# A transformer-and-experts block on one core: weights of the first group fetched early, scale and shift applied after the transpose, and the 16 copies of h2 at a block's start placed elsewhere

## The chip, the cores and the metric

The kernel runs on one core of a Trainium2 chip. TensorE (PE) multiplies, VectorE (DVE) and ScalarE (ACT) work on tiles in on-chip memory, GpSimd (POOL) starts the gathers, and SyncE (SP) starts all other transfers in the order in which they stand in its program. The metric is device microseconds of one execution, lower is better.

## The reference, cut to what matters

The block has one layer, a sequence of 1024 rows, width 1024, all in float32:

```python
mod = jax.nn.silu(c) @ w_ada + b_ada
shift1, scale1, gate1, shift2, scale2, gate2 = jnp.split(mod, 6, axis=-1)
h = rmsnorm(x, norm1_g) * (1 + scale1) + shift1
proj = h @ w_in          # stick-breaking q|k|v, sliding-window q|k|v, two gates
x = x + gate1 * (merged @ w_out)
h2 = rmsnorm(x, norm2_g) * (1 + scale2) + shift2
x = x + gate2 * peer_ffn(h2, ...)   # per row and head (8): top 16 of 16384 experts
return rmsnorm(x, final_g)

# peer_ffn, per block of 128 rows
act = gelu(einsum('td,thkd->thk', h2, expert_u[experts]))
out = einsum('thk,thkd->td', gate * act, expert_v[experts])
```

## The kernel before, in words

There are two kinds of work. The **mixer** (everything up to h2 and the scores of the experts' keys) runs over three groups of 2, 3 and 3 blocks of 128 rows. The stages of a group are called H (norm, modulation, transposes), V, QK and SB (four pairs of heads of the stick-breaking branch), SWP and SW (the window branch), MG (the gated merge, eight tiles of weights w_mg), OUT (w_out, gate1, h2) and PREP (eight heads of w_q and sub-keys sk, whose scores pick the experts).

The **expert stream** runs over 8 blocks of 128 tiles each, 1024 in all. A tile is one gather (line 530) of 128 rows of 2048 floats, 1 MB, into a ring of 10 slots. For each tile DVE forms 128 dot products with a copy of h2 (line 1411). For each quad of 4 tiles ACT takes gelu (1100) and spreads the weights over `dg` (1106), and PE sums (880) into the PSUM pair VACC. That sum, counted by `vs_done`, frees four slots, and POOL may start gathers again. A tile is 32 rows of the block by 4 experts, so `h2rep` holds in its part c the rows 32c to 32c+31 of h2, four times over the partitions. It is made anew for each block from `h2cur` in 16 steps, c = 0 to 3 by i = 0 to 3 (a quarter of the width each), each four matmuls of PE (866) and one copy of ACT (1084), which wait for each other step by step because both use one half of PSUM bank MISC. The first dot product of a block with part c needs the four copies of that c. `publish` (848, 1068, 1070) turns the picked experts into indices and gates, 32 tiles at a time, through the other half of MISC. `final` (1421 to 1431) takes a block's sum out of VACC.

Every engine's program is one straight list. It is made by `interleave`, which merges streams by the number that each `yield` gives: in the expert stream this number is the tile's, in the mixer it comes from `Plan`. Group 0 of the mixer lies at negative numbers, so it runs ahead of the first tile; groups 1 and 2 are mixed into the tiles from 0 on. A wait in one stream holds up all that stands behind it on that engine.

The modulation vector is computed in three rounds (546) from `w_ada`, 8 MB each, that go through the ring's memory, before the ring is in use. Rows scale1 and shift1 go out to HBM and come back spread over 128 partitions, and DVE applies them to the rows (1164, 1165) ahead of the transposes (564).

Of the kernel before, what the change touches and what calls it, by code (L numbers as in the profile page):

```python
# [185 lines left out]
def build(nc, x, c8, w_ada, b_ada, g1, g2, gf, w_v, w_qk, w_sw, sinks, w_mg, w_out, w_q, sk, uv, consts,  # L186
          x1_dram, h2_dram, mods_dram, k_dram, v_dram, s_dram, out):
    with ExitStack() as ctx:
# [72 lines left out]
        wqk = [rows(X0, 2 * KT, P), rows(L0, 2 * KT, P)]  # L261
# [3 lines left out]
        wsw = rows(W0, 6 * KT, P).rearrange("p (a k) n -> p a k n", a=6)  # L265
# [14 lines left out]
        wq = [rows(W0 + 2048 * i, 2 * KT, P).rearrange("p (a k) n -> p a k n", a=2) for i in range(2)]  # L280
        skt = [rows(W0 + 4096 + 256 * i, 2, NKEYS) for i in range(2)]
# [9 lines left out]
        in_rows1, in_rows2, in_rowsf = sem("in_rows1"), sem("in_rows2"), sem("in_rowsf")  # L291
# [3 lines left out]
        in_wqk = [sem("in_wqk0"), sem("in_wqk1")]  # L295
# [45 lines left out]
        with nc.Block() as block:  # L341
            @block.sync
            def _(sp):
                def start():
# [28 lines left out]
                def mixer(g):  # L373
# [1120 lines left out]
```

## Time and profile before

| | us |
|---|---|
| median of 3 runs (lowest, highest) | 3668.83 (3667.49, 3670.41) |
| the profiled execution, own time | 3687.68 |
| its span, first to last instruction | 3685.9 |
| busy: PE, weight loads, DVE, ACT, POOL | 2249.2, 996.8, 2036.1, 1144.6, 1121.7 |
| gathers started | 1024 |
| moved by DMA in all | 1276.13 MB, mean 346 GB/s |

Only one profile exists; its own time stands 18.85 us above the median of the runs. Idle time of an engine is shown in brackets with what ended it.

### The profile page before, as it was taken

To read this page: it belongs to the slowest core of one execution; us is meant where nothing else is said; L and a number is where in the kernel's file an instruction comes from. 1 tells how busy PE (TensorE), PEld (TensorE's weight loads), DVE (VectorE), ACT (ScalarE), POOL (GpSimd) and SP (SyncE) were. 2 spreads that over 40 slices of the span, in tenths; PEclk is the share of its full clock that TensorE was granted. 3 is DMA by queue.
4 is the path that set the end of the run, shared out by engine and by line. 5 is a ranking of instruction groups with operands and counts; after the bars stand their busy time and mean duration, and the time that the engine had idled before them with its cause. 6 is when DMAs were issued, how large, how long until landed. Compare 5 with 4: busy or idle time off the path is not lost.

```text
span 3685.9 us, 35795 instructions
## 1 busy us (share of the span) xinstructions
PE 2249.2 (61%) x11240; PEld 996.8 (27%) x11240; DVE 2036.1 (55%) x4768; ACT 1144.6 (31%) x3633; POOL 1121.7 (30%) x1033
## 2 busy tenths in 40 slices
PE   4678766875987856777667877684433343334333
PEld 2466623333443422223233332241000000000000
DVE  1011445657456455677577665656566656665644
ACT  1210124634213233666634213222222222222221
POOL 0000112332223323344233333333344434433432
PEclk8889868887988978888787988796555555655565
DMA  6424558888799998999899998999799989997998
GB/s 262 169 77 160 188 215 315 330 346 320 316 392 384 373 397 327 370 399 400 318 385 371 421 422 328 393 420 420 309 415 421 421 315 421 421 421 307 421 421 336
DMA packets 196264, 1276.13 MB, mean 346 GB/s; under 512 B 21261, under 2 KB 38701, under 8 KB 54633
## 3 DMA queue, kind: packets, MB, share of 16 engines
q0 software_dynamic: 147616, 1074.03, 71.8%
q1 hardware_dynamic: 48456, 199.80, 14.1%
q8 instruction: 89, 1.46, 0.2%
q14 instruction: 103, 0.84, 0.1%
HBM read 1249.35 MB, written 24.40 MB: 346 GB/s over the span
## 4 chain that ended last, share of the span: by engine, by line
PE 38%; DMA 33%; ACT 10%; issue 10%; DVE 6%; POOL 1%; another core or an unknown queue 1%; SPq 0%; POOLq 0%; DVEq 0%; ACTq 0%
DMA arena<-in_uv,idx_r 25%; PE pb L880 12%; PE pb L600 4%; PE pb L665 3%; ACT dg L1106 3%; PE pb L866 3%; PE pb L685 2%; PE pb L629 2%; ACT L104 2%; PE pb L603 2%; DVE arena L1411 2%; DMA arena<-in_w_q 2%; POOL arena L530 1%; PE pb L759 1%; DMA arena<-in_w_out 1%
## 5 line engine op out<-in xcount | busy, mean ns | idle before, releaser
L530 POOL DMA_INDIRECT arena<-in_uv,idx_r x1024 | 1118.6, 1092 | 2536.6 <-PE pb L880 1857.3
L1411 DVE CUSTOM_DVE_ANT_0 arena<-arena 128x1024 f32<-128x1024 f32 x1024 | 1247.8, 1221 | 719.9 <-DMA arena<-in_uv,idx_r 713.1
L880 PE MATMUL pb<-arena,dg 128*32 128x512 f32 x4096 | 745.1, 865 | 892.0 <-ACT dg L1106 842.6
L880 PEld LDWEIGHTS pb<-arena,dg 128*32 128x32 f32 x4096 | 134.6, 138 | 1395.5 <-ACT dg L1106 1033.7
L1100 ACT ACTIVATE gl<-dots 128x4 f32<-128x4 f32 x256 | 52.3, 204 | 1044.8 <-DVE dots L1411 1021.1
L665 PE MATMUL pb<-arena 128*128 128x384 f32 (+1 forms) x768 | 252.9, 487 | 57.3 <-issue 38.0
L104 ACT ACT_TABLE_LOAD x176 | 225.8, 1283 | 141.6 <-DVE dots L1411 68.4
L600 PE MATMUL pb<-arena 128*128 128x384 f32 (+1 forms) x768 | 241.5, 471 | 22.1 <-DMA arena<-in_w_mg 22.1
L1106 ACT ACTIVATE dg<-ig,gl 128x32 f32<-128x32 f32 x1024 | 245.1, 310 | 8.3
L1095 ACT ACTIVATE ig<-istack,gate_r 128x32 f32<-128x32 f32 x1024 | 241.5, 308 | 0.0
L665 PEld LDWEIGHTS pb<-arena 128*128 128x128 f32 x768 | 154.7, 206 | 150.3 <-issue 80.9
L600 PEld LDWEIGHTS pb<-arena 128*128 128x128 f32 x768 | 149.5, 198 | 117.5 <-issue 53.3
L866 PE MATMUL pb<-arena,ident 128*32 128x256 f32 x1024 | 106.7, 498 | 95.8 <-ACT arena L1084 87.1
L685 PE MATMUL pb<-arena 128*128 128x384 f32 (+1 forms) x384 | 127.4, 490 | 44.7 <-DMA arena<-in_w_qk 44.7
L629 PE MATMUL pb<-arena 128*128 128x512 f32 x256 | 121.6, 629 | 50.5 <-DMA arena<-in_w_out 47.7
L1277 DVE SCALAR_TENSOR_TENSOR arena<-pb,arena 128x384 f32<-128x384 f32 (+2 forms) x120 | 51.4, 470 | 153.0 <-ACT arena L1033 148.4
L603 PE MATMUL pb<-arena 128*128 128x384 f32 (+1 forms) x384 | 116.0, 454 | 0.0
L685 PEld LDWEIGHTS pb<-arena 128*128 128x128 f32 x384 | 77.7, 208 | 97.9 <-DMA arena<-in_w_qk 47.3
L713 PE MATMUL pb<-arena,tri 128*128 128x384 f32 (+2 forms) x240 | 93.5, 483 | 16.2 <-DVE arena L1277 15.1
L1084 ACT ACTIVATE arena<-pb 128x256 f32<-128x256 f32 x128 | 49.1, 384 | 147.3 <-PE pb L866 141.7
L1237 DVE SCALAR_TENSOR_TENSOR arena<-arena,pb 128x384 f32<-128x384 f32 (+1 forms) x48 | 24.3, 507 | 125.5 <-PE pb L603 125.2
L727 PE MATMUL pb<-arena 128*64 128x384 f32 (+2 forms) x240 | 67.0, 517 | 41.7 <-ACT arena L1041 39.1
(153 smaller groups left out, 2239.9 us busy)
## 6 DMA issues: line engine op xcount, KB each, us to landing
arena<-in_w_mg SPq DMA_DIRECT2D x24, 1536.0 KB
arena<-in_w_ada SPq DMA_DIRECT2D x12, 2048.0 KB, 17.7
arena<-in_w_q SPq DMA_DIRECT2D x24, 1024.0 KB
arena<-in_uv,idx_r POOLq DMA_INDIRECT x1024
arena<-in_w_qk SPq DMA_DIRECT2D x12, 1024.0 KB
arena<-in_w_out SPq DMA_DIRECT2D x3, 4096.0 KB, 16.3
arena<-in_w_sw SPq DMA_DIRECT2D x3, 3072.0 KB, 13.4
arena<-in_x SPq DMA_DIRECT2D x16, 512.0 KB, 20.8
```

The source lines that it names most:

```text
L104: self.act.add_instruction(mybir.InstLoadActFuncSet(name=self.nc.get_next_instruction_name(), act_func_set_id=table, engine=mybir.EngineTy ...
L530: pool.indirect_dma_start(ring[:, i % RING, :], None, uv, bass.IndirectOffsetOnAxis(ap=idx_r[:, b % 2, 4 * n + c:4 * n + c + 1], axis=0)). ...
L600: m = pe.matmul(bank, wmg[ft % 2][:, q * KT + k, :], hT[:, k, 0:T], start=(k == 0), stop=(k == KT - 1))
L603: m = pe.matmul(bank, wmg[ft % 2][:, 16 + (q - 2) * 4 + k, :], y[:, k, 0:T], start=(k == 0), stop=(k == 3))
L629: m = pe.matmul(pb[:, BGB + 2 * (j % 2) + i, :], merged[:, k, j * P:(j + 1) * P], wout[:, k, i * HALF:(i + 1) * HALF], start=(k == 0), sto ...
L665: m = pe.matmul(pb[:, BGB + p, 0:T], wq[h % 2][:, p, k, :], h2T[:, k, 0:T], start=(k == 0), stop=(k == KT - 1))
L685: m = pe.matmul(pb[:, BGB + i, 0:T], wqk[p % 2][:, i * KT + k, :], hT[:, k, 0:T], start=(k == 0), stop=(k == KT - 1))
L866: x_ = pe.matmul(pb[32 * q:32 * q + 32, MISC, 256:512], selector(c), h2cur[:, 256 * i:256 * i + 256], start=True, stop=True)
L880: m = pe.matmul(pb[32 * c:32 * c + 32, VACC + i, :], dg[:, STEP * n // 4 % 2, c, :], ring[:, (STEP * g + c - first) % RING, D + i * HALF:D ...
L1095: op = act.activation(ig[:, half, first + c], istack[:], ACT.Copy, scale=gate_r[:, b % 2, STEP * n + c:STEP * n + c + 1])
L1106: op = act.activation(dg[:, half, first + c], ig[:, half, first + c], ACT.Copy, scale=gl[:, a + c:a + c + 1])
L1411: dve.tensor_tensor_reduce(u, h2rep[:, c, :], u, 1.0, 0.0, ALU.mult, ALU.add, dots[:, i % 8:i % 8 + 1]).then_inc(dots_done, 1)
```

## The change

- Weights of group 0 go to places in the ring's memory (`RINGO + ...`), which is empty until the first gather, and are fetched by `first_weights` and `start`: w_v and w_qk 0 to 2 at the start, w_sw, two w_mg, w_out during the pairs, a third w_mg, w_q and sk at SW. For groups 1 and 2 the homes are as before.
- w_ada comes in halves by k, x between them in round 0. Rounds 1 and 2 of the modulation stand one pair earlier on PE.
- scale1 and shift1 are transposed on PE into a small tile `cols`. ACT scales the rows by the norm's factor (three copies of 1024), and the evacuation of the transposes applies scale and shift: four instructions of 128 columns in place of one copy of 512, on ACT and on DVE. The row loads of scale1 and shift1 go in all three groups.
- Scores for the first top-16 are copied on DVE out of `ssb`, not through HBM.
- For block 0, h2rep is loaded by four DMAs from HBM in stage OUT; its 16 steps are gone.
- For blocks 1 to 7 the 16 steps have other numbers, on PE -2.9 + 1.5c + 0.37i and on ACT -2.4 + 1.5c + 0.37i from the block's first tile (before: -3.6 and -3.5, + c + 0.1i). DVE's `final` stands ahead of the next block's first dot product, not behind it.

```diff
                     yield -2000
...
+                    for k in range(2):
+                        for c in range(2):
+                            ada(0, k, c)
+                        if k == 0:
+                            for j in range(SIZE[0]):
+                                sp.dma_start(xt[:, j, :], x[j * P:(j + 1) * P, :]).then_inc(in_x[j], 16)
+                    sp.dma_start(f(W0, 4096), w_v).then_inc(in_wv, 16)
+                    for p in range(3):
+                        sp.dma_start(f(qk_home(0, p), 2048), w_qk[p]).then_inc(in_wqk[p], 16)
...
+                def first_weights():
+                    yield at("QK", 0, 0, 0.3)
+                    sp.wait_ge(v_mm, SIZE[0])
+                    sp.dma_start(f(qk_home(0, 3), 2048), w_qk[3]).then_inc(in_wqk[3], 16)
+                    yield at("QK", 0, 2, -1)
+                    sp.wait_ge(ada_mm, 3)
+                    sp.dma_start(f(sw_home(0), 6144), w_sw).then_inc(in_wsw, 16)
+                    sp.wait_ge(qk_mm, 2)
+                    sp.dma_start(alibi, consts[:, 2 * P + TOPK + 32:2 * P + TOPK + 32 + TABLE]).then_inc(in_alibi, 16)
+                    merge_weights(0, 0)
+                    merge_weights(0, 1)
+                    yield at("QK", 0, 3)
+                    sp.wait_ge(qk_mm, 6)
+                    sp.dma_start(f(out_home(0), 8192), w_out).then_inc(in_wout, 16)
+                    yield at("SW", 0, 0)
+                    sp.wait_ge(sw_mm, 6)
+                    merge_weights(0, 2)
+                    query_weights(0, 1)
...
                 def blocks():
-                    for b in range(NB):
+                    yield at("OUT", 0, 0, 16.5)
+                    sp.wait_ge(h2_st[0], 16)
+                    sp.wait_ge(mods_out, 128)
+                    for q in range(4):
+                        sp.dma_start(h2rep[32 * q:32 * q + 32, :, :], h2_dram[0:P, :].rearrange("(c t) n -> t c n", c=4)).then_inc(in_rep, 16)
+                    for b in range(1, NB):
                         yield TILES * b - 24
...
-                        yield at("H", 0, 0, -2) if r == 0 else at("QK", 0, 2 * r - 1, -0.01)
+                        yield at("H", 0, 0, -2) if r == 0 else at("QK", 0, r - 1, -0.01)
...
-                                yield TILES * b - 3.6 + c + 0.1 * i if b else -2
+                                yield TILES * b - 2.9 + 1.5 * c + 0.37 * i
...
-                                yield TILES * b - 3.5 + c + 0.1 * i if b else -2
+                                yield TILES * b - 2.4 + 1.5 * c + 0.37 * i
...
+                    for j in range(GB):
+                        act.activation(xt[:, j, :], xt[:, j, :], ACT.Copy, scale=stats[:, 8 + j:9 + j]).then_inc(h_rows, 1)
...
+                        for k in range(4):
+                            op = act.activation(hT[:, k, j * P:(j + 1) * P], pb[:, BGB + 2 * (j % 2), k * P:(k + 1) * P], ACT.Identity,
+                                                scale=cols[:, 2 + k // 4, k % 4:k % 4 + 1], bias=cols[:, k // 4, k % 4:k % 4 + 1])
...
-                        link(dve.scalar_tensor_tensor(out=xt[:, j, :], in0=xt[:, j, :], scalar=stats[:, 8 + j:9 + j], in1=sc1_row, op0=ALU.mult, op1=ALU.mult))
-                        dve.tensor_tensor(xt[:, j, :], xt[:, j, :], sh1_row, ALU.add).then_inc(h_rows, 1)
...
                     for b in range(NB):
-                        yield TILES * (b + 1) + 0.9
+                        yield TILES * (b + 1) - 0.05
                         dve.wait_ge(vs_done, STEPS * (b + 1))
```

**SP in group 0, from pair 1's k on.** v_scratch to arena is the values of a pair (vp), which its scores wait for. Before:

```order
L418 DMA k_scratch<-arena 128x256
L423 DMA arena<-in_w_sw 128x6144
L424 DMA arena<-in_consts 128x1536
L431 DMA arena<-in_w_mg 128x3072 x8
L370 DMA arena<-mods_scratch 128x1024
L371 DMA arena<-in_gf 128x1024
L434 DMA arena<-in_w_out 128x8192
```

and of the change:

```order
L476 DMA k_scratch<-arena 128x256
L408 DMA arena<-in_w_sw 128x6144
L410 DMA arena<-in_consts 128x1536
L431 DMA arena<-in_w_mg 128x3072 x2
L469 DMA arena<-v_scratch 128x256
L476 DMA k_scratch<-arena 128x256
L469 DMA arena<-v_scratch 128x256
L415 DMA arena<-in_w_out 128x8192
L476 DMA k_scratch<-arena 128x256
L431 DMA arena<-in_w_mg 128x3072
L434 DMA arena<-in_w_q 128x2048
```

w_sw and two w_mg now stand ahead of the values of pair 2, and w_out behind those of pair 3.

**PE at the start of block 7**, 880 being the sums before (961 now), 866 the steps of h2rep (947 now) and 848 the publishing (929 now). Before:

```order
L880 MATMUL pb<-arena,dg 32x512 x56
L866 MATMUL pb<-arena,ident 32x256 x16
L880 MATMUL pb<-arena,dg 32x512 x8
L866 MATMUL pb<-arena,ident 32x256 x16
L848 MATMUL pb<-picks,ident 32x16 x16
L866 MATMUL pb<-arena,ident 32x256 x32
L880 MATMUL pb<-arena,dg 32x512 x64
```

and of the change, 4 matmuls to a step:

```order
L961 MATMUL pb<-arena,dg 32x512 x64
L947 MATMUL pb<-arena,ident 32x256 x12
L929 MATMUL pb<-picks,ident 32x16 x16
L947 MATMUL pb<-arena,ident 32x256 x28
L961 MATMUL pb<-arena,dg 32x512 x8
L947 MATMUL pb<-arena,ident 32x256 x24
L961 MATMUL pb<-arena,dg 32x512 x56
```

Before, 4 steps stood ahead of the sum of the last quad but one and 12 behind it, all ahead of the last quad's sum. Now none stands ahead of the former; 10 stand ahead of the last quad's sum and 6 behind it.

**ACT at the same place**, 1084 being the copies of the steps (1176 now), 1100 and 1106 the last quad's gelu and spreading (1192 and 1198 now). Before:

```order
L1084 ACTIVATE arena<-pb 128x256 x4
L104 ACT_TABLE_LOAD
L1062 ACTIVATE best<-best 128x32
L1084 ACTIVATE arena<-pb 128x256
L1095 ACTIVATE ig<-istack,gate_r 128x32 x4
L1084 ACTIVATE arena<-pb 128x256 x3
L1068 ACTIVATE idx_r<-pb 128x4x8
L1070 ACTIVATE gate_r<-pb 128x4x8
L1084 ACTIVATE arena<-pb 128x256 x8
L104 ACT_TABLE_LOAD
L1100 ACTIVATE gl<-dots 128x4
L1106 ACTIVATE dg<-ig,gl 128x32 x4
```

and of the change:

```order
L1176 ACTIVATE arena<-pb 128x256 x3
L1162 ACTIVATE idx_r<-pb 128x4x8
L1164 ACTIVATE gate_r<-pb 128x4x8
L1176 ACTIVATE arena<-pb 128x256 x4
L104 ACT_TABLE_LOAD
L1192 ACTIVATE gl<-dots 128x4
L1198 ACTIVATE dg<-ig,gl 128x32 x4
L1176 ACTIVATE arena<-pb 128x256 x4
L1187 ACTIVATE ig<-istack,gate_r 128x32 x4
L1176 ACTIVATE arena<-pb 128x256 x3
L1205 ACTIVATE arena,stats<-arena 128x1024
```

The last quad's gelu stood behind all 16 copies; it now stands behind 7, and 9 follow it.

## Rows read from the trace of the kernel before

**Rows 1.** The page, chain that ended last: share of the span by engine.

```profile
PE 38%; DMA 33%; ACT 10%; issue 10%; DVE 6%; POOL 1%; another core or an unknown queue 1%; SPq 0%; POOLq 0%; DVEq 0%; ACTq 0%
```

**Rows 2.** Windows: busy us by engine, then clock (1 is full), DMA share, GB/s.

```profile
474.00:532.00 58.00, 26.92 (x173) 8.99 (x172) 20.84 (x45) 17.21 (x43) 0.00 (x0) 0.54 0.29 117
2700.00:2800.00 100.00, 36.01 (x192) 6.30 (x192) 67.66 (x156) 22.95 (x94) 38.05 (x38) 0.57 1.01 421
3335.00:3435.00 100.00, 38.82 (x228) 7.07 (x224) 58.95 (x137) 29.09 (x99) 33.01 (x32) 0.52 0.85 341
```

**Rows 3.** Timeline of PE to 540 us: start, us, what, [idle before <-releaser].

```profile
29.32 9.54 PE L546 MATMUL pb<-arena,cb 128*32 128x512 f32 x64 [29.32 <-DMA arena<-in_w_ada]
...
58.75 15.41 PE L576 MATMUL pb<-arena 128*128 128x512 f32 x32 [0.87 <-DVE arena L1168]
80.81 9.49 PE L685 MATMUL pb<-arena 128*128 128x256 f32 x32 [6.65 <-DMA arena<-in_w_qk]
...
134.94 9.73 PE L685 MATMUL pb<-arena 128*128 128x256 f32 x32 [13.39 <-DMA arena<-in_w_qk]
...
185.60 16.90 PE L759 MATMUL pb<-arena 128*128 128x256 f32 x64 [10.03 <-DMA arena<-in_w_sw]
...
245.17 9.22 PE L600 MATMUL pb<-arena 128*128 128x256 f32 x32 [6.35 <-DMA arena<-in_w_mg]
...
257.68 7.07 PE L600 MATMUL pb<-arena 128*128 128x256 f32 x32
...
344.29 29.74 PE L629 MATMUL pb<-arena 128*128 128x512 f32 x64 [13.93 <-DMA arena<-in_w_out]
...
390.78 9.79 PE L665 MATMUL pb<-arena 128*128 128x256 f32 x32 [6.36 <-DMA arena<-in_sk]
...
531.70 5.89 PE L576 MATMUL pb<-arena 128*128 128x512 f32 x12
```

**Rows 4.** Source view of the four first w_ada loads: us from issue to landing.

```profile
L354 SPq DMA_DIRECT2D arena<-in_w_ada x4: 423/432/432, 4.9 to 6.4; - x4
...
DMA to landing us min/median/max: 9.5/16.2/22.8
```

**Rows 5.** DMA view: two groups of weights, KB each, median us to landing.

```profile
arena<-in_w_mg SPq DMA_DIRECT2D x24, 1536.0 KB
...
arena<-in_w_sw SPq DMA_DIRECT2D x3, 3072.0 KB, 13.4
```

**Rows 6.** Timeline between group 0 and group 1, DVE, PE and ACT.

```profile
419.60 0.29 DVE L1309 MAX8 vals<-arena 128x8 f32<-128x128 f32 x1 [34.44 <-DMA arena<-s_scratch]
...
443.68 0.49 PE L848 MATMUL pb<-picks,ident 128*32 128x16 f32 x32 [4.15 <-DVE picks L1385]
...
481.07 1.06 ACT L904 ACTIVATE arena<-arena 128x1024 f32<-128x1024 f32 x1 [6.27 <-DMA arena<-in_x]
...
508.43 0.38 ACT L1084 ACTIVATE arena<-pb 128x256 f32<-128x256 f32 x1 [1.20 <-PE pb L866]
...
508.83 1.28 ACT L104 ACT_TABLE_LOAD   x1
```

**Rows 7.** Source view of the copies into h2rep: ns min/median/max, first and last start.

```profile
L1084 ACT ACTIVATE arena<-pb x128: 358/384/387, 484.7 to 3345.2; 128x256 f32<-128x256 f32 x128
```

**Rows 8.** Timeline at the start of block 7, POOL, ACT and PE.

```profile
3309.95 0.94 POOL L530 DMA_INDIRECT arena<-in_uv,idx_r  x1 [4.96 <-PE pb L880]
...
3317.64 0.38 ACT L1084 ACTIVATE arena<-pb 128x256 f32<-128x256 f32 x1 [1.35 <-DVE dots L1411]
...
3326.18 1.88 POOL L530 DMA_INDIRECT arena<-in_uv,idx_r  x1 [11.56 <-PE pb L880]
...
3348.18 3.64 PE L880 MATMUL pb<-arena,dg 128*32 128x512 f32 x16 [3.01 <-ACT dg L1106]
...
3352.66 0.94 POOL L530 DMA_INDIRECT arena<-in_uv,idx_r  x1 [20.88 <-PE pb L880]
...
3367.77 1.57 POOL L530 DMA_INDIRECT arena<-in_uv,idx_r  x1 [9.62 <-PE pb L880]
```

More of the change, by code:

```diff
@@ L279, in build, with qk_home, sw_home, mg_home @@
         h2T = merged
[L280 to L281 removed]
         qp = rows(W0 + 4608, 2, TMAX)
         ssb = [f(W0 + 4608 + 2 * TMAX * (i + 1), 2 * TMAX).rearrange("p (b q n) -> p b q n", b=GMAX, q=2) for i in range(2)]
+        def qk_home(g, p):
+            return (X0, RINGO + 16384, RINGO + 18432, L0)[p] if g == 0 else (X0, L0)[p % 2]
+        def sw_home(g):
+            return RINGO if g == 0 else W0
+        def mg_home(g, ft):
+            return RINGO + (6144, 9216, 0)[ft % 3] if g == 0 else W0 + 3072 * (ft % 2)
+        def mg_turn(g, ft):
+            if g == 0:
+                return ft % 3, ft // 3 + 1
+            return ft % 2, 3 + KT // 2 * (g - 1) + ft // 2 + 1
+        def out_home(g):
+            return RINGO + 12288 if g == 0 else A0
+        def q_home(g, h):
+            return RINGO + 3072 if (g, h) == (0, 1) else W0 + 2048 * (h % 2)
+        def sk_home(g, h):
+            return (RINGO + 5120 if g == 0 and h < 2 else W0 + 4096) + 256 * (h % 2)
         dve_steps, pool_steps = sem("dve_steps"), sem("pool_steps")
@@ L357, in mods @@
                 def mods():
-                    for r in range(3):
-                        yield at("H", 0, 0, -0.5) if r == 0 else at("QK", 0, 2 * r - 1, 0.5)
+                    for r in range(1, 3):
+                        yield at("H", 0, 0, 1) if r == 1 else at("QK", 0, 0, 0.6)
+                        sp.wait_ge(ada_mm, r)
+                        for k in range(2):
+                            for c in range(2):
+                                ada(r, k, c)
+                        yield at("QK", 0, r - 1, 0.5)
@@ L506, in finals @@
                         sp.dma_start(out[b * P:(b + 1) * P, :], yfin).then_inc(stored, 16)
-                interleave(start(), mods(), mixer(0), parked(0), keys(), blocks(), finals(), *[s for g in range(1, GROUPS) for s in (mixer(g), parked(g))])
+                interleave(start(), mods(), first_weights(), mixer(0), parked(0), keys(), blocks(), finals(), *[s for g in range(1, GROUPS) for s in (mixer(g), parked(g))])
                 sp.wait_ge(stored, 16 * NB)
@@ L548, in modulation @@
                         m.then_inc(ada_mm, 1)
+                        if r == 0:
+                            yield at("V", 0, 0, -0.5)
+                            pe.wait_ge(md_done, 1)
+                            for i in range(4):
+                                m = pe.transpose(pb[:, MISC, i * P:(i + 1) * P], md[:, 0, i * P:(i + 1) * P], ident[:])
+                            m.then_inc(cols_mm, 1)
                 def mixer(g):
@@ L1328, in one @@
                         n = CHUNKS * b + m
-                        dve.wait_ge(in_tk[n % 2], 16 * (n // 2 + 1))
+                        if n == 0:
+                            dve.wait_ge(pr_se, 4)
+                            for h in range(2):
+                                step.mark(dve.tensor_copy(tk[:, 0, 256 * h:256 * h + 256].rearrange("p (q n) -> p q n", q=2), ssb[h][:, 0]))
+                            step.hold()
+                            dve.sem_inc(tk_first, 1)
+                        else:
+                            dve.wait_ge(in_tk[n % 2], 16 * ((n + 1) // 2))
                         for h in range(2):
```

204 lines of the change are left out of this document (115 added, 89 removed).

## The prediction

> **What bounds the kernel now.** The chain that ended last comes first [rows 1]: PE holds 38% of the span, DMA 33%, ACT 10% and issue 10%. So there isn't one bound, and the windows [rows 2] tell where each rules. From 2700 to 2800 us the 16 DMA engines are full (share 1.01, 421 GB/s) and PE is busy 36 of 100 us: the stream of gathers is the bound. In the 100 us from 3335, the start of block 7, the same stream moves 341 GB/s: 80 of 421 are missing, which is 19 us. From 474 to 532 us, between group 0 of the mixer and group 1, DMA moves 117 GB/s and PE has 27 busy us of 58: neither is full. Ahead of that lies group 0, a chain through PE with hardly any gather. Its timeline on PE [rows 3] shows six waits for weights, in the brackets: 6.65 and 13.39 us for w_qk, 10.03 for w_sw, 6.35 for w_mg, 13.93 for w_out, 6.36 for w_q and sk, and 29.32 for the first w_ada. Their sum without the last is 56.7 us. The matmuls behind such a wait are slower too: 32 of form 128x256 take 9.22 us at 245.17 and 7.07 us at 257.68.
>
> What ends at 531.70, when group 1's first V matmul starts, sets the time of all that follows, since the program from there on is the old one but for the starts of the blocks. So I count what moves that point, then the block starts. All sums are made against the profiled execution's 3687.7 us, which stands 18.9 us above the median of the runs, and are then moved down by that.
>
> **Start.** The four first w_ada loads are issued from 4.9 to 6.4 us and land 9.5 to 22.8 us later [rows 4], at 14.4 and 29.2: 4.93 us for each 2 MB. Now two come first (19.4), then 1 MB of x (21.8), then two more (31.7). The 64 passes of round 0 took 9.54 us [rows 3]; the second half of them, after a wait, I give 6 us: 37.5. Then come 20 transposes and the evacuations, without the trip of scale1 and shift1 over HBM and without DVE's two passes over each tile. V started at 58.75; it can't start ahead of 37.5, and were nothing saved behind the matmuls it would start at 57.4 (19.9 us behind them, as before). I take 45, nearer to the first, since the trip and the passes were most of the 19.9. Gain 13.7 us.
>
> **The six waits.** The loads now stand ahead of the work by whole stages, so the 56.7 us go if they land in time. The clock gives back 2.4 (80.81), 2.7 (134.94), 2.8 (185.60, against twice 7.07), 2.2 (245.17) and 1.4 (344.29, 29.74 against four times 7.07): 11.5. The first head of PREP stays slow, PE being idle ahead of it anyway.
>
> **New waits on the same path.** Round 1 of w_ada is issued at 37.5 behind w_v and three w_qk (5 MB, until 44.0) and lands at 63.7; V ends at 60.4, and the first half of the round covers the rest: nothing. QK of pair 0 starts at 67.3. Round 2 is issued at about 70 and its last load lands 22.8 us later, at 92.8; PE is through pair 0 (7.1 and some 9 us) and half the round at 87.0. Cost 5.8 us and 1.0 of clock: 6.8. SP then issues w_sw, 768 KB of constants and two w_mg [rows 5], 6912 KB or 16.6 us at the rate of [rows 4], at about 106, and the values of pair 2 behind them at 113.5, when pair 1 ends. They land at about 125; QK of pair 2 is through at 120.2. Cost 4.7 us. w_out lands during pair 3 and SWP, which need nothing of SP then. Group 0 is shorter by 13.7 + 56.7 + 11.5 - 6.8 - 4.7 = 70.4 us.
>
> The Trainium skill says in DMA: Bandwidth & Descriptors, section Queues, rings and completion order, that on each DMA engine the descriptors of one ring are taken in order. That speaks against early fetching, and the four landings one after another [rows 4] agree. Its rule makes a rival below.
>
> **Between the groups.** The scores of the first top-16 came over HBM: DVE began at 419.60 after 34.4 us, and PE waited 4.15 us to publish [rows 6]. The copy on DVE starts it some 10 us sooner against the heads: 4.2 us go. Then the squares of group 1 start at 481.07, but the norm's factor stood behind the 16 copies for block 0, the last at 508.43; V came 50.6 us behind the squares. Now: squares 3.8, the factor 3.5 with its table load of 1.28, a first scaled tile 1.1, transposes and evacuations of two tiles 5, the first quad's gelu on ACT ahead of the third evacuation 2.5, its sum on PE ahead of V 3.6: 19.5. Gain 31 us; not under 24.1 (484.7, the first copy [rows 7], to 508.8), not over 36. The evacuation in four parts and the three scalings on ACT are in this. The four loads of h2rep, 2 MB or 5 us, fall into OUT's second half, where SP has little. DVE's new wait for the k stores, ACT's for h2's stores and for DVE's copy are for things that end a stage ahead: nothing. POOL's first gather waits for the second head instead of round 2, and for its indices long after. Point 531.70 moves by 70.4 + 4.2 + 31 = 105.6 us.
>
> **Starts of blocks 1 to 7.** In block 7 [rows 8] POOL starts quads at 3309.95, 3326.18, 3352.66 and 3367.77, where the full stream has one each 9.95 us (4 MB at 421 GB/s). The 16 copies run from 3317.64 to 3345.2 [rows 7, 8], about 1.6 us a step, with publishing (3 us) amid them; only then come gelu and the last quad's sum, 3348.18 to 3351.82. Now: the last quad but one isn't held up, its gathers start at 3319.9. The first step follows that sum at 3321.1, the publishing comes after three, the seventh copy ends at 3334.2; table, gelu and spreading take 2.7. But PE has steps 8 and 9 ahead of the sum, which wait for copies behind the spreading: 3 us more, so the sum runs from 3339.8 to 3343.4 and its gathers start at 3344.3, 8.4 us sooner. Six steps are left, with an `ig` group and the square of `final` amid the copies: copy 16 ends at about 3353.7, and the fourth dot product of the block, which needs it, ends at 3355. Before it ended at some 3358.8. So most of the 8.4 is given back: the quad behind starts 3 to 5 us sooner. I take 4 us; the bounds are nothing (the last copy decides) and 19 (all that is missing in [rows 2]). Times 7: 28. The stall that goes from ACT's gelu appears at DVE, ahead of the dot product with part 3.
>
> **Less traffic.** Rows scale1 and shift1 for groups 1 and 2, 4 times 0.5 MB, go from a stretch where DMA is mostly full: 2.1 MB at 421 GB/s, 5 us.
>
> **Sum.** 105.6 + 28 + 5 = 138.6. 3687.7 - 138.6 = 3549.1; less 18.9: **3530 us**.
>
> **Rivals.**
> - *The block starts give nothing.* The 16 steps are as many as before and chained by the same bank, and the last one decides when the quad behind can be summed. For it: the 8.4 us above shrink to 4 within a quad. Against it: in [rows 8] two of three intervals are long only because of ACT's order. 3668.8 - 110.6 = 3558.
> - *They give much.* If the gathers that start 8.4 us sooner keep DMA full, and each start loses 9 us, not 19: 10 times 7. 3668.8 - 110.6 - 70 = 3488. Against it: the last copy.
> - *SP's ring holds up group 0.* If small loads and stores wait for a full 16.6 us twice more than counted (k of pair 2, values of pair 3, h2), 33 us come back: 3563. For it: the first four loads land strictly in turn, 4.9 us each [rows 4]. Against it: SP issues such loads mostly a stage ahead. The section of DMA: Bandwidth & Descriptors in the Trainium skill named above has this as its rule.
> - *Slower.* DVE's `final` now stands ahead of the first dot product of a block, and waits for the last quad's sum; all top-16 steps and mixer work of DVE wait behind it, and PE's mixer matmuls for them. It was one dot product later before. At 110.6 / 7 = 15.8 us more for each start the gain is gone; with 18 us the time is 3684. Against it: DVE was idle there before too, since part 1 wasn't copied.
>
> **How the numbers follow.** Forecast 0.55 (its own range 3505 to 3553, from 24 to 36 between the groups and 0 to 7 at each start), nothing at the starts 0.20, much there 0.13, SP's ring 0.09, slower 0.03. From 3485 to 3585 about 0.85 is held. A difference under 0.2% is about what a measurement can't tell; faster 0.96, same 0.01, slower 0.03.
>
> **What would show it.** In the profile after: V of group 0 at about 45 us, SWP at about 148, MG at about 199 and the first PREP head at about 320, each without a wait for DMA; a wait of some 5 us each in round 2 and at pair 2's scores; group 1's V at about 426. At block 7, intervals of POOL near 10, 24 and 19 us where 16, 26 and 15 stood, and DVE waiting for ACT's last copies. I'm wrong if SWP starts behind 165, if group 1's V starts behind 445, or if the block starts still move 341 GB/s or move over 390.

## Result and the profile after

The changed kernel takes 3530.88 us (median of 3 runs, 3529.61 to 3536.16) against 3668.83 before: ratio 0.9619, 95% interval 0.9592 to 0.9647, 138 us less. Its profiled execution took 3529.61 us, its span 3527.8. In the chain of work that ended last PE stands at 40% and DMA at 35%, as mixed as before [rows 1]:

```profile
PE 40%; DMA 35%; ACT 10%; issue 9%; DVE 4%; POOL 1%; SPq 0%; POOLq 0%; DVEq 0%; ACTq 0%
```

The timeline of PE up to group 1's first V matmul answers to [rows 3]:

```profile
19.54 5.79 PE L615 MATMUL pb<-arena,cb 128*32 128x512 f32 x32 [19.54 <-DMA arena<-in_w_ada]
32.04 6.37 PE L615 MATMUL pb<-arena,cb 128*32 128x512 f32 x32 [6.70 <-DMA arena<-in_w_ada]
...
44.18 15.67 PE L651 MATMUL pb<-arena 128*128 128x512 f32 x32 [3.43 <-DVE arena L1260]
...
65.61 3.64 PE L615 MATMUL pb<-arena,cb 128*32 128x512 f32 x32 [2.20 <-DMA arena<-in_w_ada]
...
96.01 5.11 PE L615 MATMUL pb<-arena,cb 128*32 128x512 f32 x32 [6.45 <-DMA arena<-in_w_ada]
...
129.26 0.49 PE L778 MATMUL pb<-arena 64*128 64x128 f32 x4 [4.76 <-DMA arena<-v_scratch]
...
154.07 14.08 PE L840 MATMUL pb<-arena 128*128 128x256 f32 x64
...
205.19 7.17 PE L676 MATMUL pb<-arena 128*128 128x256 f32 x32 [0.69 <-ACT arena L1048]
...
289.47 27.70 PE L706 MATMUL pb<-arena 128*128 128x512 f32 x64 [1.13 <-DVE arena L1335]
...
328.45 10.16 PE L744 MATMUL pb<-arena 128*128 128x256 f32 x32 [0.88 <-DVE arena L1360]
...
434.60 5.71 PE L651 MATMUL pb<-arena 128*128 128x512 f32 x10
```

L615 is w_ada's round (two halves each), L651 V, L840 SWP, L676 MG, L706 OUT and L744 the first head of PREP; the counts are the profile's records, two for each matmul of the program. V stands at 44.18 (was 58.75), SWP at 154.07 (185.60), MG at 205.19 (245.17), the first head at 328.45 (390.78) and group 1's V at 434.60 (531.70). No bracket holds w_qk, w_sw, w_mg, w_out, w_q or sk any more. Behind the start, three waits for DMA are left in group 0: 2.20 us for round 1 of w_ada, 6.45 for round 2, and 4.76 for the values of pair 2.

SP's own timeline shows what the last two wait for. It has when each load is issued and for how long SP is at it:

```profile
71.67 2.09 SPq L383 DMA_DIRECT2D arena<-in_w_ada  x4
...
109.06 0.43 SPq L408 DMA_DIRECT2D arena<-in_w_sw  x1
...
110.02 1.01 SPq L431 DMA_DIRECT2D arena<-in_w_mg  x2
117.42 0.33 SPq L469 DMA_DIRECT2D arena<-v_scratch  x1
```

Round 2 is issued from 71.67 to 73.76 us and PE's second half of it starts at 96.01, 22.3 us behind. The values of pair 2 (L469) are issued at 117.42, behind w_sw, the constants and two w_mg (109.06 to 111.03), and PE gets them at 129.26, 11.8 us later. The Trainium skill (DMA: Bandwidth & Descriptors, section Queues, rings and completion order) has descriptors of a ring taken in order; the trace agrees, and in e6 below, with the order turned round, the wait is gone.

Windows at the three places of [rows 2] (busy us by engine, clock, DMA share, GB/s):

```profile
377.00:435.00 58.00, 32.95 (x203) 25.16 (x202) 31.29 (x104) 21.52 (x53) 9.48 (x10) 0.75 0.71 288
2600.00:2700.00 100.00, 34.32 (x188) 6.33 (x192) 66.73 (x163) 23.21 (x95) 43.37 (x40) 0.59 1.01 421
3188.00:3288.00 100.00, 38.45 (x248) 7.52 (x248) 68.89 (x165) 28.40 (x103) 38.53 (x37) 0.69 0.92 370
```

In the middle of a block the stream is as before, 421 GB/s. Between the groups DMA moves 288 GB/s where it moved 117. At the start of block 7 it moves 370 where it moved 341, at a granted clock of 0.69 instead of 0.52. These two windows don't begin at the same point of the start, though; over the 100 us from the quad of 3173.59 on (before: 3326.18) it is 364 GB/s for 326, at 0.69 for 0.54, and the second profile of the kernel before (c0) has 340 there. The start itself, POOL, PE, ACT and DVE in one, answers to [rows 8]:

```profile
3162.68 0.94 POOL L598 DMA_INDIRECT arena<-in_uv,idx_r  x1 [4.96 <-PE pb L961]
...
3172.53 1.08 PE L947 MATMUL pb<-arena,ident 128*32 128x256 f32 x8
...
3173.59 0.94 POOL L598 DMA_INDIRECT arena<-in_uv,idx_r  x1 [6.21 <-PE pb L961]
...
3176.63 0.45 PE L929 MATMUL pb<-picks,ident 128*32 128x16 f32 x32 [0.59 <-ACT arena L1176]
...
3177.15 0.23 ACT L1162 ACTIVATE idx_r<-pb 128x32 uint32<-128x32 f32 x1 [0.67 <-PE pb L929]
...
3183.32 0.38 ACT L1176 ACTIVATE arena<-pb 128x256 f32<-128x256 f32 x1 [1.20 <-PE pb L947]
...
3185.25 0.96 ACT L1198 ACTIVATE dg<-ig,gl 128x32 f32<-128x32 f32 x4
...
3188.11 1.08 PE L947 MATMUL pb<-arena,ident 128*32 128x256 f32 x8 [0.50 <-ACT arena L1176]
...
3188.96 3.16 PE L961 MATMUL pb<-arena,dg 128*32 128x512 f32 x16
...
3192.20 1.23 DVE L1526 TENSOR_TENSOR arena<-pb,arena 128x1024 f32<-128x1024 f32 x1 [14.41 <-PE pb L961]
...
3192.97 0.94 POOL L598 DMA_INDIRECT arena<-in_uv,idx_r  x1 [14.38 <-PE pb L961]
...
3193.07 0.64 PE L947 MATMUL pb<-arena,ident 128*32 128x256 f32 x8 [0.51 <-ACT arena L1176]
...
3198.51 0.38 ACT L1176 ACTIVATE arena<-pb 128x256 f32<-128x256 f32 x1 [0.76 <-PE pb L947]
...
3199.71 1.21 DVE L1516 CUSTOM_DVE_ANT_0 arena<-arena 128x1024 f32<-128x1024 f32 x1
...
3209.75 1.76 POOL L598 DMA_INDIRECT arena<-in_uv,idx_r  x1 [11.26 <-PE pb L961]
```

POOL's quads stand 10.9, 19.4 and 16.8 us apart; before it was 16.2, 26.5 and 15.1. The last quad's sum starts at 3188.96, straight behind two steps (3188.11), and the last of the 16 copies at 3198.51. DVE's `final` (L1526) waits 14.41 us for that sum. The dot product that needs the last copy (L1516) follows at 3199.71, 0.8 us behind the copy's end, and has no wait for it: DVE was at the three before it until then.

To compare runs, one figure sums up a start: the time from the gather of the 6th tile ahead of a block's first to that of the 18th behind it. At the full stream these 24 tiles take 6 times 9.95 us, 59.7. By POOL's timelines, us, for blocks 1 to 7:

| run | 1 | 2 | 3 | 4 | 5 | 6 | 7 | sum | V(1) on PE | span |
|---|---|---|---|---|---|---|---|---|---|---|
| before | 98.7 | 100.2 | 95.7 | 101.7 | 85.8 | 82.9 | 85.7 | 650.7 | 531.70 | 3685.9 |
| before, again (c0) | 98.5 | 98.9 | 93.4 | 102.0 | 82.1 | 81.5 | 82.9 | 639.4 | 531.29 | 3671.8 |
| after | 93.9 | 96.5 | 89.1 | 96.5 | 72.4 | 70.7 | 73.9 | 593.1 | 434.60 | 3527.8 |
| e1 | 93.9 | 96.0 | 87.6 | 95.8 | 74.3 | 71.4 | 75.4 | 594.4 | 532.87 | 3627.5 |
| e2 | 98.5 | 105.5 | 94.4 | 105.1 | 82.3 | 81.1 | 82.2 | 649.3 | 436.15 | 3577.1 |

The two spans before and after differ by 158.1 us: 97.1 at V(1) (the first V matmul of group 1), 57.6 at the starts, 3.4 elsewhere. The second profile of the kernel before, nearer to its median, gives 144.0: 96.7, 46.3 and 1.0.

### The profile page after: what moved, and what is told of

It is laid out like the page before. It is cut to its first block, busy times and chain, and to the rows that moved or that the text cites. A ratio compares the mean times of both kernels' runs of the same rounds, so it can differ in the third digit from the quotient of the medians.

```text
span 3527.8 us, 35548 instructions
## 1 busy us (share of the span) xinstructions
PE 2206.6 (63%) x11116; PEld 985.4 (28%) x11116; DVE 2024.6 (57%) x4779; ACT 1151.1 (33%) x3649; POOL 1119.7 (32%) x1033
## 2 busy tenths in 40 slices
DMA packets 197214, 1274.27 MB, mean 361 GB/s; under 512 B 21192, under 2 KB 38632, under 8 KB 54048
## 3 DMA queue, kind: packets, MB, share of 16 engines
q1 hardware_dynamic: 49408, 197.96, 14.6%
## 4 chain that ended last, share of the span: by engine, by line
PE 40%; DMA 35%; ACT 10%; issue 9%; DVE 4%; POOL 1%; SPq 0%; POOLq 0%; DVEq 0%; ACTq 0%
DMA arena<-in_uv,idx_r 26%; PE pb L961 13%; PE pb L676 5%; PE pb L744 4%; ACT dg L1198 3%; PE pb L706 3%; DMA arena<-in_w_q 2%; ACT L104 2%; PE pb L679 2%; DMA arena<-in_w_ada 2%; PE pb L947 2%; PE pb L765 2%; PE pb L840 2%; DVE arena L1516 1%; PE pb L651 1%
## 5 line engine op out<-in xcount | busy, mean ns | idle before, releaser
L1516 DVE CUSTOM_DVE_ANT_0 arena<-arena 128x1024 f32<-128x1024 f32 x1024 | 1249.6, 1222 | 741.5 <-DMA arena<-in_uv,idx_r 733.1
L961 PE MATMUL pb<-arena,dg 128*32 128x512 f32 x4096 | 737.3, 857 | 891.8 <-ACT dg L1198 891.6
L744 PE MATMUL pb<-arena 128*128 128x384 f32 (+1 forms) x768 | 254.5, 490 | 57.6 <-issue 44.7
L676 PE MATMUL pb<-arena 128*128 128x384 f32 (+1 forms) x768 | 238.1, 465 | 16.3 <-DMA arena<-in_w_mg 15.7
L744 PEld LDWEIGHTS pb<-arena 128*128 128x128 f32 x768 | 155.2, 207 | 152.4 <-issue 92.6
L676 PEld LDWEIGHTS pb<-arena 128*128 128x128 f32 x768 | 147.2, 195 | 110.6 <-issue 46.0
L706 PE MATMUL pb<-arena 128*128 128x512 f32 x256 | 119.4, 618 | 38.5 <-DMA arena<-in_w_out 34.9
L947 PE MATMUL pb<-arena,ident 128*32 128x256 f32 x896 | 83.7, 451 | 50.4 <-ACT arena L1176 46.6
L793 PE MATMUL pb<-arena,tri 128*128 128x384 f32 (+2 forms) x240 | 94.1, 486 | 14.6 <-DVE arena L1373 14.5
L765 PEld LDWEIGHTS pb<-arena 128*128 128x128 f32 x384 | 73.9, 198 | 76.5 <-DMA arena<-in_w_qk 24.9
L1062 ACT ACTIVATE arena<-pb 128x384 f32<-128x384 f32 (+1 forms) x48 | 21.7, 453 | 208.4 <-PE pb L676 208.4
## 6 DMA issues: line engine op xcount, KB each, us to landing
arena<-in_w_mg SPq DMA_DIRECT2D x24, 1536.0 KB, 10.9
arena<-in_w_q SPq DMA_DIRECT2D x24, 1024.0 KB, 11.7
```

The costliest lines, as they stand in the source:

```text
L676: m = pe.matmul(bank, wmg[:, q * KT + k, :], hT[:, k, 0:T], start=(k == 0), stop=(k == KT - 1))
L706: m = pe.matmul(pb[:, BGB + 2 * (j % 2) + i, :], merged[:, k, j * P:(j + 1) * P], wout[:, k, i * HALF:(i + 1) * HALF], start=(k == 0), sto ...
L744: m = pe.matmul(pb[:, BGB + p, 0:T], wq[:, p * KT + k, :], h2T[:, k, 0:T], start=(k == 0), stop=(k == KT - 1))
L765: m = pe.matmul(pb[:, BGB + i, 0:T], wqk[:, i * KT + k, :], hT[:, k, 0:T], start=(k == 0), stop=(k == KT - 1))
L947: x_ = pe.matmul(pb[32 * q:32 * q + 32, MISC, 256:512], selector(c), h2cur[:, 256 * i:256 * i + 256], start=True, stop=True)
L961: m = pe.matmul(pb[32 * c:32 * c + 32, VACC + i, :], dg[:, STEP * n // 4 % 2, c, :], ring[:, (STEP * g + c - first) % RING, D + i * HALF:D ...
```

## The experiments

Three sets, each on a chip of its own, with the kernel before beside them: it took 3674.17 us (c0 to e3), 3687.15 (e4 to e7) and 3669.86 (a0 and e9 to e11). So ratios are compared, and times only within a set. The changed kernel stands in the third set alone (a0); e1 to e7 are compared with it across chips. The changed kernel itself has 0.9619 on one chip and 0.9599 on another (a0), so that ratios of two sets differ by 0.2% without a cause in the kernel.

**c0: the kernel before once more.**

> The kernel before, unchanged, for a second profile. Its first profiled execution took 3687.7 us, 18.9 us above the median of its runs, and the changed kernel's 3529.6, at its median of 3530.9; so the two traces differ by 158 us and the medians by 138. If the 19 us are a slower execution, a second profile has a span of about 3669 and some stage of the gather stream is shorter; if the profiler itself costs this kernel 19 us, it is near 3686 again.

Measured: 3672.68 us, ratio 0.9992 [0.9979, 1.0005]. So the comparison itself is good to 0.1%. Its trace has the sum of the starts 11.3 us under that of the first profile. ACT's copy of the indices in the publishing tells the two apart; the first profile, then c0, both at block 7:

```profile
3332.54 0.23 ACT L1068 ACTIVATE idx_r<-pb 128x32 uint32<-128x32 f32 x1 [2.88 <-remote]
```

```profile
3320.29 0.22 ACT L1068 ACTIVATE idx_r<-pb 128x32 uint32<-128x32 f32 x1 [0.67 <-PE pb L848]
```

`remote` is something that the profile puts to another core or an unknown queue. Such waits of this copy stand in the first profile (17 of them) and in all four of the second set (e4 to e7, 20 to 24), and in none of the other nine, the changed kernel's among them. Their cause is open. The sums of the starts fit: e4, e5 and e6 have 604.8, 603.4 and 600.0 us, 7 to 12 more than the changed kernel, though none of their edits touches these starts. That the wait makes this difference is likely, not shown.

**e1: the starts alone.** The kernel before with the new places of the 16 steps and of `final`.

```
- PE   yield TILES * b - 3.6 + c + 0.1 * i if b else -2
+ PE   yield TILES * b - 2.9 + 1.5 * c + 0.37 * i if b else -2
- ACT  yield TILES * b - 3.5 + c + 0.1 * i if b else -2
+ ACT  yield TILES * b - 2.4 + 1.5 * c + 0.37 * i if b else -2
- DVE  yield TILES * (b + 1) + 0.9
+ DVE  yield TILES * (b + 1) - 0.05
```

> The kernel before with one part of the change: the places of the 16 steps of blocks 1 to 7 on PE and ACT, and DVE's final ahead of the next block's first dot product. By the two traces the stretch from the quad at -6 to the quad at +18 of a block is shorter by 4.8, 3.7, 6.6, 5.2, 13.4, 12.2 and 11.8 us in blocks 1 to 7, 58 us in all: 3611. By the forecast, 4 us each: 3641. If the last of the 16 copies decides and the starts give nothing: 3669.

Measured: 3626.70 us, 47.5 less, ratio 0.9858 [0.9831, 0.9886]. The starts sum to 594.4 us, as in the full change, and V(1) stays at 532.87. The starts are worth more than the 28 us of the forecast.

**e2: the starts undone.** The changed kernel with the three old places.

> The changed kernel with the starts of blocks 1 to 7 as before (places of the 16 steps, and final behind the first dot product). If the parts add up as in the traces: 3531 + 58 = 3589. By the forecast's 4 us each: 3559. If the starts give nothing: 3531.

Measured: 3578.89 us, 95.3 less than before, ratio 0.9728 [0.9703, 0.9753]. The starts sum to 649.3, V(1) is at 436.15. The two parts add up to within 5 us: 47.5 and 95.3 make 142.8, and the whole change gave 138 on its chip and 141.4 as a0.

**e3: `final` behind the first dot product again, the steps spread as in the change.** One line, `TILES * (b + 1) + 0.9`.

> The changed kernel with DVE's final again behind the first dot product of the next block; the 16 steps stay where the change has them. Theory: the steps' places make the gain and final is worth the one dot product of 1.2 us that stands in its way, at most 1 us a block: 3531 to 3539. Rival: final's early place frees VACC sooner for the next sum and makes a good part of it: over 3545.

Measured: 3522.07 us, ratio 0.9576 [0.9553, 0.9599]; the changed kernel has 0.9619 and, as a0, 0.9599. The expectation, 3531 to 3539, was missed on the low side. The starts sum to 592.2. So the early `final` is not what gained: that rival's mechanism is in the trace (14.41 us), but not its price. What e1 gained is then the work of the steps. In e3 the dot product with the last part waits for the last copy at all seven starts (1.10 to 4.97 us), so what DVE gets back there it waits again. Whether `final` behind is a little faster, by some 0.4%, stays open; e10 and e11 below don't agree on it.

**e4: block 0's copies by 16 steps again, with the prefetch and all else kept.**

```
- sp.dma_start(h2rep[32 * q:32 * q + 32, :, :], h2_dram[0:P, :].rearrange("(c t) n -> t c n", c=4)).then_inc(in_rep, 16)
...
+ yield TILES * b - 2.9 + 1.5 * c + 0.37 * i if b else -2
```

> The changed kernel with block 0's copy of h2 made again by the 16 steps on PE and ACT between group 0 and group 1, in place of four DMAs. The squares of group 1 stand ahead of the 16 copies on ACT and the norm's factor behind them, as before. If the stretch is worth the 16 steps: 24 to 26 us, 3556. Rival: the gathers' first wave is not yet summed by then anyway, or the transfer of x decides, and it costs under 10 us: under 3541.

Measured: 3562.63 us, ratio 0.9676 [0.9657, 0.9695]. ACT's timeline of this kernel:

```profile
417.57 1.06 ACT L980 ACTIVATE arena<-arena 128x1024 f32<-128x1024 f32 x1
...
418.62 0.36 ACT L1173 ACTIVATE arena<-pb 128x256 f32<-128x256 f32 x1
...
442.40 0.38 ACT L1173 ACTIVATE arena<-pb 128x256 f32<-128x256 f32 x1 [1.20 <-PE pb L942]
...
444.10 0.20 ACT L985 ACTIVATE stats<-stats 128x3 f32<-128x3 f32 x1
```

Group 1's squares (L980) are done, then come 16 copies (L1173) from 418.62 to 442.78, and only then the norm's factor (L985). V(1) stands at 458.74, 24.1 us behind the change, and the span is 29.9 longer, its starts 11.7 (see c0); by the ratio it is 21 to 28 us. The lower bound of the forecast for this gap, 24.1 from [rows 7], is what the copies took.

**e5: w_sw and w_out loaded only when their stage begins, into the same empty ring.**

```
+ yield at("SWP", g, 0, -1)
+ sp.wait_ge(pv_done, chunk(g, PAIRS - 1, 0, 0) + NC[g])
+ sp.dma_start(f(sw_home(g), 6144), w_sw).then_inc(in_wsw, 16)
...
+ sp.wait_ge(mg_mm, 4 * KT * (g + 1))
+ sp.dma_start(f(out_home(g), 8192), w_out).then_inc(in_wout, 16)
```

> The changed kernel with w_sw and w_out of group 0 fetched at their old places in the program (behind the last pair, and behind the last merge), into their new homes. Theory: the two waits come back with the slower clock behind them, 10.0 + 2.8 + 13.9 + 1.4 = 28 us, less 2 to 5 us since the values of pair 2 no longer wait behind w_sw: 3554 to 3559. Rival: later stages take up part of it: under 3545.

Measured: 3563.13 us, ratio 0.9667 [0.9644, 0.9690]. PE's timeline has both old waits back, 9.98 and 14.13 us where [rows 3] has 10.03 and 13.93:

```profile
158.89 16.84 PE L840 MATMUL pb<-arena 128*128 128x256 f32 x64 [9.98 <-DMA arena<-in_w_sw]
...
309.97 30.07 PE L706 MATMUL pb<-arena 128*128 128x512 f32 x64 [14.13 <-DMA arena<-in_w_out]
```

V(1) comes at 456.58, 22.0 us behind the change, less than the 24.1 of the two waits, since pair 2's values aren't held up now. The span is 38.3 us longer, of which 10.3 lie at the starts (603.4 against 593.1), where nothing was changed but the copy's wait of c0 is back; by the ratio it is 18 to 25 us, about what V(1) lost.

**e6: SP issues pair 2's values ahead of w_sw, the constants and w_mg.**

```
- yield at("QK", 0, 2, -1)
+ yield at("QK", 0, 2, -0.9)
```

> The changed kernel with one swap on SP: the values of pair 2 are issued ahead of w_sw, the constants and two w_mg, not behind them. PE waited 4.76 us for these values in the profile. If SP's ring order is the cause, that wait goes and w_sw still comes in time: 3526. If something else delays the values, or w_sw comes late now: 3531 or more.

Measured: 3541.56 us, ratio 0.9618 [0.9602, 0.9635], no different from the change. In the trace the wait of 4.76 us is gone and V(1) comes at 429.80, 4.8 us sooner; the span is 3.4 us shorter. The wait has the cause that was named. What it is worth, 0.1%, can't be told in the time.

**e7: all blocks' copies by DMA, like block 0's.** 16 loads of 128 KB for each block in place of the 16 steps.

```
- sp.dma_start(h2cur, h2_dram[b * P:(b + 1) * P, :]).then_inc(in_h2, 16)
+ for c in range(4):
+     yield TILES * b - 3.4 + c
+     sp.wait_ge(dots_done, TILES * b - 3 + c)
+     for q in range(4):
+         sp.dma_start(h2rep[32 * q:32 * q + 32, c, :], h2_dram[b * P + 32 * c:b * P + 32 * c + 32, :]).then_inc(in_part[c], 16)
```

> The changed kernel with h2rep of blocks 1 to 7 loaded from HBM by 16 DMAs of 128 KB each, part c as soon as the last dot product with it is done; the 16 steps of PE and ACT and the load of h2cur are gone. If the chain of 16 steps is what the starts still lose (72 us where 59.7 would be the full stream, six quads at 9.95), they lose only the 1.5 MB more of traffic, 3.6 us each: 5 to 9 us gained a start, 3470 to 3495. Rival: the parts stand behind 8 MB of gathers in the DMA engines and arrive as late as the copies: 3531 or more.

Measured: 3566.44 us, ratio 0.9684 [0.9670, 0.9700]: slower than the change, and the expectation failed. The start of block 7 in its timelines:

```profile
3202.10 4.15 SPq L566 DMA_DIRECT2D arena<-h_scratch  x8
...
3205.30 0.94 POOL L601 DMA_INDIRECT arena<-in_uv,idx_r  x1 [6.19 <-PE pb L964]
...
3207.03 6.73 SPq L566 DMA_DIRECT2D arena<-h_scratch  x8
...
3219.07 0.94 POOL L601 DMA_INDIRECT arena<-in_uv,idx_r  x1 [8.77 <-PE pb L964]
...
3229.73 1.23 DVE L1519 CUSTOM_DVE_ANT_0 arena<-arena 128x1024 f32<-128x1024 f32 x1 [3.65 <-DMA arena<-h_scratch]
...
3236.01 1.23 DVE L1519 CUSTOM_DVE_ANT_0 arena<-arena 128x1024 f32<-128x1024 f32 x1 [4.77 <-DMA arena<-h_scratch]
...
3246.26 1.57 POOL L601 DMA_INDIRECT arena<-in_uv,idx_r  x1 [22.16 <-PE pb L964]
```

The gathers behind the last sum do start 13.8 us after the quad before instead of 19.4, but the next quad comes 27.2 us later instead of 16.8. SP is at the 16 loads from 3202.10 to 3213.76, and DVE waits for the third and fourth parts until 3229.73 and 3236.01: the last load lands some 22 us after its issue, while the gathers fill the same DMA engines (how these share between the two queues no row here tells). And the loads bring 10.9 MB more (1285.15 against 1274.27 in the DMA view), 26 us at 421 GB/s, with the stream full. The starts sum to 632.1, 39 more than in the change and 32 more than in e6 of the same chip, which has the wait of c0 too. Of these 32, 26 lie at blocks 1 and 2, beside mixer work, and 3.0 to 3.5 at each of blocks 5 to 7, no more than the 3.7 us that 1.5 MB takes at 421 GB/s; blocks 3 and 4 together are 3.4 shorter. V(1) comes 5.9 us later than in the change. The rival on record named the late parts.

**a0: the changed kernel once more**, beside e9 to e11.

> The changed kernel once more, on the chip on which the next three run: its ratio to the kernel before should lie within 0.3% of 0.9619. It is what the ratios of e9, e10 and e11 are compared with, since a chip was seen on which the kernel before takes 13 us more.

Measured: 3528.49 us, ratio 0.9599 [0.9576, 0.9622]. Starts 594.5, V of group 1 as in the first trace.

**e9: steps 8 and 9 behind the last quad's sum on PE.** PE's place gets `+ (0.75 if c == 2 and i < 2 else 0)`.

> Steps 8 and 9 stand behind the last quad's sum on PE instead of ahead of it. In block 7 of the changed kernel the sum starts at 3188.96 us, though the weights were spread by 3186.1: it stood behind the two steps. Theory A, the quad's gathers decide: the sum and its gathers start 2.9 us sooner at each start and half of it or more is kept, 7 times 1.5 to 2.9 us, ratio 0.3 to 0.55% under that of a0. Theory B, the last copy decides: copies 9 to 16 come 3.5 us later, the fourth dot product of the block with them, and nothing is gained or 1 us lost at each start: ratio equal to a0 or up to 0.2% above.

Measured: 3521.49 us, ratio 0.9586 [0.9568, 0.9605]; not told apart from a0. Its trace decides between the theories:

```profile
3168.47 0.94 POOL L598 DMA_INDIRECT arena<-in_uv,idx_r  x1 [5.85 <-PE pb L961]
...
3179.87 3.64 PE L961 MATMUL pb<-arena,dg 128*32 128x512 f32 x16 [1.42 <-ACT dg L1198]
...
3184.35 0.94 POOL L598 DMA_INDIRECT arena<-in_uv,idx_r  x1 [10.52 <-PE pb L961]
...
3192.58 0.38 ACT L1176 ACTIVATE arena<-pb 128x256 f32<-128x256 f32 x1 [0.76 <-PE pb L947]
...
3193.11 1.22 DVE L1516 CUSTOM_DVE_ANT_0 arena<-arena 128x1024 f32<-128x1024 f32 x1 [1.95 <-ACT arena L1176]
...
3203.36 1.57 POOL L598 DMA_INDIRECT arena<-in_uv,idx_r  x1 [13.50 <-PE pb L961]
```

The sum now starts 11.4 us behind the quad of 3168.47 (15.4 before) and its gathers 15.9 (19.4). But the last copy starts at +24.1 where it was +24.9, and the quad after that comes at +34.9 for +36.2: of 3.5 to 4 us 1.3 are left. In the mean of the seven starts, against a0, the gathers behind the sum go from +21.8 to +19.7, the last copy from +29.0 to +29.4, and the quad after that stays at +39.8 (594.4 us in all, 594.5 in a0). The last copy takes it back: theory B. DVE shows it: in e9 the dot product with the last part waits for the copy at all seven starts (1.93 to 5.41 us). In the changed kernel it does so at blocks 1 to 3 alone (3.12, 1.81 and 1.46 us); at blocks 4 to 7 the other chain, from the last sum through `final` and three dot products, ends 0.3 to 0.8 us behind the last copy and decides. The two end almost together, so that shortening one gave nothing.

**e10 and e11: e3 and e6 together, and both with e9.**

> Both single edits together: the values of pair 2 issued ahead of round 2's successors on SP (e6), and DVE's final behind the first dot product (e3). By their traces e6 takes 4.8 us off the start of group 1, and e3 took 8 us off the median of the runs while its trace's block starts were the same to 1 us. If both are real the ratio is 0.2 to 0.35% under a0's; if e3's gain was the chip's or the run's, 0.1% under.

> e10 with the steps of e9. If the three don't depend on each other, its ratio is a0's less the differences of e9 and e10: 0.4 to 0.9% under a0's by theory A of e9, 0 to 0.35% under by theory B.

Measured: e10 3510.28 us, ratio 0.9566 [0.9545, 0.9588]; e11 3518.36 us, 0.9589 [0.9570, 0.9609]. e10 has the lowest ratio of all, 0.33% under a0, as it was to be if both gains are real, but the intervals touch, and e11, which holds the same two edits, is 0.10% under. Its trace has 10.4 us less of span, of which 6.0 lie ahead of the first dot product (412.0 against 418.0) and 3.6 at the starts (590.9). e9's steps add nothing to it.

Not tested by themselves are the waits for w_qk, w_mg, w_q and sk, the scale and shift behind the transposes, and the copy of scores on DVE; for them there are the traces before and after alone.

## Why the prediction was right, step by step

The mechanisms held; that the forecast of 3530 us met 3530.88 to 1 us is luck. Without the starts 110.6 us were counted and e2 has 95.3; for the starts 28 were counted and e1 has 47.5. The errors, some 15 and some 19 us, cancel. (The forecast's own range, 3505 to 3553, is also not what its two terms give: 24 for 31 between the groups and nothing for 28 at the starts make 3565.)

**Start: held.** 13.7 us were counted, 14.6 came; V stands at 44.18 for a forecast of 45.

**Six waits: held; e5 brings two of them back at their old size.** What came in their place was a little more than counted: 6.45 for 5.8 in round 2, 4.76 for 4.7 at pair 2's values, and 2.20 in round 1, where "the first half of the round covers the rest: nothing" was wrong.

**The clock's 11.5 us: held at their places; what failed is the 1.0 us for slower matmuls behind the new waits.** From V to SWP 23.7 us were to go, and 17.0 went. The window of that stretch, of the kernel before and then of the kernel after:

```profile
58.75:185.60 126.85, 87.48 (x416) 53.50 (x416) 9.22 (x29) 22.90 (x78) 0.00 (x0) 0.85 0.47 182
```

```profile
44.18:154.07 109.89, 88.34 (x417) 52.92 (x417) 9.33 (x29) 22.60 (x77) 0.00 (x0) 0.88 0.69 276
```

PE is busy 87.48 us in the one and 88.34 in the other. The matmuls of the w_qk stages take 29.3 us in place of 33.6; with SWP, the first of MG and OUT 4.3, 2.8, 2.1 and 2.0 us came for 5.1, 2.8, 2.2 and 1.4 counted. But those of w_ada in this stretch take 16.0 in place of 14.1, since the second half of round 2 is slow (5.11 where a half at full speed takes 3.64, at a granted clock of 0.50), and the scores and sums of the pairs 31.6 in place of 28.3, those behind 129.26 at a granted clock of 0.53. In e6 pair 2's run fast, but some of pair 3's are slow, where PE waited for no DMA; so not all of this is the new waits' doing. The waits themselves took 2.9 us more than counted. From SWP to MG 8.5 us went for 9.2 counted, from MG to the first head 22.4 for 23.9. Group 0 is shorter by 62.3 us; 70.4 was the forecast.

**Between the groups: held.** 35.2 us were counted from the first head to group 1's V, 34.8 came. The squares start at 414.15 and V(1) at 434.60: 20.5 us, for 19.5. e4 puts 24.1 of it down to block 0's copies alone. So V(1) moved by 97.1 us for 105.6.

**Starts: the mechanism was right, the size was not.** 4 us each and 28 together were counted; e1 measures 47.5, e2 leaves 40 to 47, the traces have 46 to 58. In blocks 5 to 7, without mixer work beside them, it is 9 to 11 us a start by c0's trace, in blocks 1 to 4 it is 2 to 6. In block 7 the three intervals of POOL make 47.1 us, where c0 has 55.2 and the first profile 57.8. The term that was sized wrong is the copies' time. I took 1.6 us for every step and 3 for the publishing. In the rows after, the steps behind the last sum come every 1.14 us, because their matmuls (8 records) take 0.64 us there and 1.08 ahead of it. The trace of the kernel before had this already: four steps behind a sum at 3322.11 take 0.61 to 0.64 us and the eight behind the publishing 1.08; 1.6 was a mean over the slow steps and the fast. And across the publishing (PE 3176.63, ACT 3177.15) PE's steps are 2.2 us apart, not 4.6: c0 has 2.2 as well, so the 3 us were the first profile's wait for `remote` and not the work of publishing. So measured from the quad of 3173.59, the sum starts at +15.4 (forecast +19.9) and copy 16 ends at +25.3 (+33.8). That the last copy gives back what the sum gains held in part: e9 shows it, but in the changed kernel DVE waits for that copy at blocks 1 to 3 alone.

**Less traffic: not seen.** 5 us were counted; what V(1) and the starts leave is 1.0 to 3.4.

**The 18.9 us** between the first profiled execution and the median were taken off at the end. c0's trace shows where 11.3 of them lay: in the block starts, with the copy of the indices that waited for `remote`. So the 19 us that [rows 2] had missing at one start were somewhat too many, and the first pair of traces overstates what the starts gave.

**The rivals.** Nothing at the starts: fallen by e1. Much there, 70: not reached, though 47.5 lies about midway between 28 and 70. SP's ring holding up group 0: fallen. The waits of 6.45 and 4.76 us were in the forecast; beyond them only the 2.20 of round 1 came, not 33. Slower: fallen by the result; e3 shows that the early `final` has no price that can be told.

## What to carry to other kernels

Weights that are loaded into a buffer that is empty anyway take away whole waits, and what is left are the loads that stand behind them in the same queue: look at each small load that is issued behind the big ones. Where work is interleaved with a chain of steps at a boundary, look for the chain that ends last, not the one that was moved: here two of them end within 1 us of each other, so that shortening one gave nothing (e3, e9). Time such a chain at both clocks, since here its steps through PE ran faster straight behind a burst of matmuls. A copy that moves from an engine to DMA is free only where DMA has room: 2 MB ahead of the first block took 24 us off the path, the same for seven blocks in the full stream cost more than it saved. And a forecast from one profile takes over what only that profile has: the 3 us of publishing weren't in the second.

## What the runs showed of the hardware

The same matmuls of a step (8 records of 128x256) take 1.08 us in the steps ahead of the last quad's sum and 0.64 behind it (PE at 3172.53 and 3193.07). The windows of these two stretches have a granted clock of 0.50 and of 1.00, the two levels of TensorE's clock (1.2 and 2.4 GHz):

```profile
3180.00:3188.50 8.50, 4.80 (x40) 1.02 (x40) 0.00 (x0) 4.25 (x11) 0.00 (x0) 0.50 0.87 353
3192.50:3200.00 7.50, 3.25 (x44) 0.79 (x40) 7.17 (x17) 3.98 (x12) 4.60 (x4) 1.00 0.70 228
```

The sum of 16 records of 128x512, 3.16 us, stands between them. In the second stretch PE is less busy than in the first, 3.25 of 7.5 us against 4.80 of 8.5, and keeps the upper level for the six steps.

Loads of 128 KB issued by SP while POOL's gathers fill the DMA engines landed some 22 us later (e7), where w_ada's four loads of 2 MB, with DMA empty, took 9.5 to 22.8 [rows 4].

Two profiles of the same kernel differ by 14 us in span, 11.3 of it at the seven block starts and 0.4 at V(1); one of them has 17 waits of ACT's copy of indices for `remote`, the other none.
